# Evictions, silu and products ahead of weight splits, and level exponentials in two instructions, in a two-layer hybrid decoder trunk

## The reference

```python
def swiglu(x, w_gu, w_down):
    a, u = jnp.split(x @ w_gu, 2, axis=-1)           # 1024 -> 2 x 2816
    return (jax.nn.silu(a) * u) @ w_down             # 2816 -> 1024

# hgrn2_mixer: 4 heads of 128, by chunks, b = cumsum of log f along the tokens
att = jnp.einsum('bhtc,bhsc,bhtsc->bhts', qt, kt, decay)      # decay = exp(b_t - b_s), s <= t
o = einsum(att, vt) + einsum(qt * jnp.exp(b), state)
new_state = state * jnp.exp(b_last) + einsum(kt * jnp.exp(b_last - b), vt)

for i in range(DEPTH):                                        # DEPTH = 2
    x = layer_norm(alpha * x + 0.5 * swiglu(x, ffn_w_gu[i, 0], ffn_w_down[i, 0]), ...)
    y = token_mix(x, w_in[i], w_out[i], ...)                  # NSA | sliding window | HGRN2
    x = layer_norm(alpha * x + y, ...)
    x = layer_norm(alpha * x + 0.5 * swiglu(x, ffn_w_gu[i, 1], ffn_w_down[i, 1]), ...)
    x = x + sigmoid(x @ ple_gate_w[i] + ple_gate_b[i]) * (p[i] @ ple_w[i])
```

## Time and profile before

| what | value |
|---|---|
| median of 3 runs | 2474.37 us (2471.06 to 2482.52) |
| profiled execution, its own time | 2477.05 us |
| its span, first to last instruction | 2475.3 us |
| TensorE busy | 2312.3 us, 93% |
| VectorE busy | 1201.9 us, 49% |
| ScalarE busy | 812.4 us, 33% |
| GpSimd busy | 162.2 us, 7% |
| mean granted TensorE clock | 0.966 of 2.4 GHz |
| moved from memory | 199.33 MB, 81 GB/s |

### The profile page before, as it was taken

The page is one execution under the profiler, slowest core; times in us unless marked ns, Lnnn a source line. Parts: engine busy times, 40 slices in busy tenths (PEclk is TensorE's granted clock), DMA queues, the critical chain, the costliest instruction groups (busy, mean ns, idle before and its releaser), DMA issues.

```text
span 2475.3 us, 26371 instructions
## 1 busy us (share of the span) xinstructions
PE 2312.3 (93%) x10523; PEld 1823.0 (74%) x10523; DVE 1201.9 (49%) x1975; ACT 812.4 (33%) x1243; POOL 162.2 (7%) x142
## 2 busy tenths in 40 slices
PE   7999998999687999999999999989997789999998
PEld 6888886787355788888778888867864567888877
DVE  4333345786766433333533333367867663333444
ACT  3222224441334422222432222244413343222223
POOL 0000020220001000012000000211100010000110
PEclk9999999999789999999999999999988999999999
DMA  4333333221202233333323333332202123333321
GB/s 141 94 94 95 92 94 84 77 68 35 73 26 64 85 94 94 92 100 94 88 80 95 96 93 88 99 89 61 71 27 69 35 64 102 94 94 98 94 85 64
DMA packets 379563, 203.15 MB, mean 82 GB/s; under 512 B 8881, under 2 KB 376625, under 8 KB 379441
## 3 DMA queue, kind: packets, MB, share of 16 engines
q1 hardware_dynamic: 379440, 201.46, 28.4%
HBM read 199.33 MB, written 2.10 MB: 81 GB/s over the span
## 4 chain that ended last, share of the span: by engine, by line
PE 82%; DVE 9%; ACT 4%; issue 3%; DMA 2%; SPq 0%; POOL 0%; DVEq 0%; ACTq 0%
PE banks L240 23%; PE banks L242 23%; PE banks L241 23%; PE banks L267 2%; PE banks L268 2%; PE banks L273 2%; PE banks L773 1%; DVE w_lo L232 1%; ACT w_hi L226 1%; DVE lev L963 1%; PE banks L1179 1%; DMA w_raw<-in_ffn_w_gu_dram 1%; PE banks L1192 1%; DVE mx L1465 1%; ACT lev L1379 1%
## 5 line engine op out<-in xcount | busy, mean ns | idle before, releaser
L232 DVE TENSOR_TENSOR w_lo<-w_raw,w_hi 128x1024 fp32r<-128x1024 f32 (+2 forms) x378 | 453.9, 1203 | 967.2 <-ACT w_hi L226 966.8
L240 PE MATMUL banks<-xhi,w_hi 128*128 128x512 f32 x1888 | 761.9, 404 | 33.0 <-DVE prod L457 13.5
L241 PE MATMUL banks<-xlo,w_hi 128*128 128x512 f32 x1888 | 751.5, 398 | 0.0
L242 PE MATMUL banks<-xhi,w_lo 128*128 128x512 f32 x1888 | 750.9, 398 | 0.0
L226 ACT ACTIVATE w_hi<-w_raw 128x1024 fp32r<-128x1024 f32 (+2 forms) x378 | 376.8, 999 | 913.9 <-PE banks L242 861.8
L240 PEld LDWEIGHTS banks<-xhi,w_hi 128*128 128x128 f32 x1888 | 358.9, 190 | 128.5 <-DVE prod L457 15.3
L242 PEld LDWEIGHTS banks<-xhi,w_lo 128*128 128x128 f32 x1888 | 358.8, 190 | 86.3
L241 PEld LDWEIGHTS banks<-xlo,w_hi 128*128 128x128 f32 x1888 | 359.1, 190 | 84.6 <-issue 1.9
L240 PE MATMUL banks<-hhi,w_hi 128*128 128x512 f32 x704 | 277.3, 394 | 0.0
L242 PE MATMUL banks<-hhi,w_lo 128*128 128x512 f32 x704 | 274.1, 389 | 0.0
L241 PE MATMUL banks<-hlo,w_hi 128*128 128x512 f32 x704 | 274.0, 389 | 0.0
(11 more groups left out here) (250 smaller groups left out, 2064.0 us busy)
## 6 DMA issues: line engine op xcount, KB each, us to landing
w_raw<-in_ffn_w_gu_dram SPq DMA_DIRECT2D x176, 512.0 KB, 3.9
w_raw<-in_ffn_w_down_dram SPq DMA_DIRECT2D x64, 512.0 KB, 4.0
w_raw<-in_w_in_dram SPq DMA_DIRECT2D x52, 512.0 KB, 4.1
w_raw<-in_ffn_w_down_dram SPq DMA_DIRECT2D x32, 384.0 KB, 3.4
w_raw<-in_w_out_dram SPq DMA_DIRECT2D x32, 256.0 KB, 2.8
w_raw<-in_ple_gate_w_dram SPq DMA_DIRECT2D x16, 512.0 KB, 4.1
w_raw<-in_cmp_k_w_dram SPq DMA_DIRECT2D x8, 512.0 KB, 4.0
w_raw<-in_cmp_v_w_dram SPq DMA_DIRECT2D x8, 512.0 KB, 4.0
```

What stands on the lines that cost most here:

```text
L232: dve.tensor_tensor(part_view(wlo, n), raw_view(split_at[n]).rearrange("p k n -> p (k n)"), part_view(whi, n), ALU.subtract).then_inc(sems ...
L240: pe.matmul(bank, w_hi, x_hi, start=first, stop=False)
L241: pe.matmul(bank, w_hi, x_lo, start=False, stop=False)
L242: return pe.matmul(bank, w_lo, x_hi, start=False, stop=last)
```

## The change

The change reorders instructions of ScalarE and VectorE, in three ways.

In the feed-forward, silu(0) stands before the splits of pieces 4 and 5, product(0) before their low splits; product(1) and hidden_lo(0) stand before the low splits of pieces 6 and 7, and hidden_hi(0) before their high splits.

In the mixer, evictions (`out`) stand before the split of the same step on both engines in all steps. ScalarE's part(0, 2), which waits for VectorE's and GpSimd's subtractions, moves from step 5 to step 6, behind the high split of piece 9.

In the mixer's part 2, ScalarE's exponential over seven levels becomes two, over four and three levels, each with a semaphore increment (lev_exp); VectorE's part 3 waits for each of them in turn, and for the queries' exponential (a2) only before its last multiplication.

```diff
             for s in range(3, UP + 3 * DT):            # ffn_act
+                if s == 3:
+                    silu(0)
+                if s == 4:
+                    hidden_hi(0)
                 for n in ahead(s):
                     split_hi(act, n0 + n)
                 if s < UP and s % 2:
-                    if s == 3:
-                        silu(0)
                     silu(s // 2)
                 if s <= UP and s % 2 == 0:
-                    if s == 4:
-                        hidden_hi(0)
                     hidden_hi(s // 2 - 1)
...
+                if s == 3:                             # ffn_dve
+                    product(0)
+                if s == 4:
+                    product(1)
+                    hidden_lo(0)
                 for n in ahead(s):
                     split_lo(dve, n0 + n)
-                if s <= UP and s % 2 == 0:
-                    if s == 4:
-                        product(0)
+                if 4 < s <= UP and s % 2 == 0:
                     product(s // 2 - 1)
                 if 5 <= s <= UP + 1 and s % 2:
-                    if s == 5:
-                        hidden_lo(0)
                     hidden_lo((s - 3) // 2)
...
-                    act.activation(l2, l2, ACT.Exp)    # in_act, part 2
+                    for l0, l1 in ((0, 4), (4, LEVELS)):
+                        l2 = lev[:, LEVELS * (h % 2) + l0:LEVELS * (h % 2) + l1, :].rearrange("p l n -> p (l n)")
+                        act.activation(l2, l2, ACT.Exp).then_inc(sems["lev_exp"], 1)
...
+                if s % 2 and s > 3:                    # in_act, steps
+                    out(s - 1)
                 for m in ahead(s):
                     if m < N_IN:
                         split_hi(act, n0 + m)
-                if s % 2 and s > 3:
-                    out(s - 1)
-                if -4 <= n < STEPS and c < 3 and h + 1 < H:
+                if -4 <= n < STEPS and c < 3 and h + 1 < H and n != -2:
                     part(h + 1, c)
+                if n == -1:
+                    part(0, 2)
                 if n == -1:
                     values_out(0)
...
-                    dve.wait_ge(*upto("a2", layer, h + 1))   # in_dve, part 3
                     projected(dve, layer, T_HQ + h)
                     for lv in range(LEVELS):
+                        if lv in (0, 4):
+                            dve.wait_ge(*upto("lev_exp", layer, 2 * h + 1 + lv // 4))
                         r = pairs(level(h, lv), lv, 1)
                         dve.tensor_tensor(r, r, pairs(proj[:, T_HQ + h, :], lv, 1), ALU.mult)
+                    dve.wait_ge(*upto("a2", layer, h + 1))
                     dve.tensor_tensor(qd_of(h), qd_of(h), proj[:, T_HQ + h, :], ALU.mult).then_inc(sems["d3"], 1)
...
+                if s % 2 == 0:                         # in_dve, steps
+                    out(s - 1)
                 for m in ahead(s):
                     if m < N_IN:
                         split_lo(dve, n0 + m)
-                if s % 2 == 0:
-                    out(s - 1)
```

More of the change, by code:

```diff
@@ L120, in build @@
                 "misc_in": 16 * 4, "aux_in": 16 * 3, "rope_in": 16 * 2, "made": 4, "out_act": 13, "out_dve": 13,
-                "a0": 4, "d0": 4, "a1": 4, "d1": 4, "d2": 4, "p2": 4, "a2": 4, "d3": 4, "c_mm": 16, "att_done": 16,
+                "a0": 4, "d0": 4, "a1": 4, "d1": 4, "d2": 4, "p2": 4, "lev_exp": 8, "a2": 4, "d3": 4, "c_mm": 16, "att_done": 16,
                 "b4_mm": 17, "b4_out": 17, "st_mm": 12, "st_out": 12, "pv_done": 16, "o_raw": 4, "sq_done": 4, "ms_mm": 4,
@@ L881, in part @@
                     act.wait_ge(*upto("p2", layer, h + 1))
-                    l2 = lev[:, LEVELS * (h % 2):LEVELS * (h % 2) + LEVELS, :].rearrange("p l n -> p (l n)")
-                    act.activation(l2, l2, ACT.Exp)
+                    for l0, l1 in ((0, 4), (4, LEVELS)):
+                        l2 = lev[:, LEVELS * (h % 2) + l0:LEVELS * (h % 2) + l1, :].rearrange("p l n -> p (l n)")
+                        act.activation(l2, l2, ACT.Exp).then_inc(sems["lev_exp"], 1)
                     act.activation(kd_of(h), kd_of(h), ACT.Exp)
```

## The result

The changed kernel takes 2438.49 us (median of 4 runs, 2430.07 to 2439.68), the kernel before 2474.52 us (4 runs, 2471.06 to 2482.52). The ratio is 0.9848, with a 95% interval of 0.9828 to 0.9868: 1.5% faster. The forecast was 2437 us.

What follows compares the result with a forecast made beforehand. TensorE, busy 93% of the span, was taken as the bound, with its idle time and lower clock to gain. 21.4 + 14.8 + 1.6 - 0.2 = 37.6 us off the median 2474.37 us gave 2437 us, range 2430 to 2452.

Steps and rivals of the forecast that it cites:

- Feed-forward openings, 21.4 us: Four feed-forward openings: TensorE's waits for the product (13.5 us) and the slow pieces behind them (7.9 us) go.
- clock term: Feed-forward openings: the four pieces behind the waits, slow at a lowered clock, return to 5.58 us; 7.9 us gained.
- Mixer openings, 14.8 us: Both layers' mixer openings: TensorE's waits for piece 5's eviction (6.1 and 4.3 us) and the slow pieces behind them go.
- The later waits, 1.6 us: Later in each mixer: TensorE's 0.81 us wait for an eviction behind a low split goes; 1.6 us for both layers.
- VectorE's lead, 0.2 us taken and 5.6 us kept for the range: Mixers: the next head's subtractions may run beside GpSimd's, returning up to 2.8 us of waits per layer; 0.2 us taken.
- The exponentials in two instructions, nothing: Mixer part 2: splitting the level exponential is worth about nothing; the first head's part 3 is just on time without it.
- The prediction's check on the span: Span shorter by 5 us at the first feed-forward stage's end, by 13 to 14 us in layer 0's attention heads.
- Rival C: Attention heads: shifted phase drops the clock for good, 77 us lost per layer; at half of it 2514 us; chance 0.02.
- A: Openings: waits go but the clock falls nevertheless, so 12.3 us of slow pieces stay; 2449 us; chance 0.10.
- D: A moved instruction waits for something as late as before; with the feed-forward part void, 2458 us; chance 0.06.
- B: Mixers: VectorE becomes the bound and sets the pace, 5.8 us lost per layer; 2448 us; chance 0.10.

Runs made afterwards that it cites:

- one that takes back the clock term alone: Kernel before, with 20 matmuls of constants run by TensorE during each feed-forward opening's wait for the product: 2465.82 us, ratio 0.9963.
- one that removes both: Kernel before with only the feed-forward part of the change, the mixer as before: 2453.34 us, ratio 0.9903.
- the other three kernels that have the wait: Kernel before with the mixer's new order alone (2456.41 us), two exponentials alone (2474.85 us), or piece 5's eviction alone moved ahead (2465.16 us).
- both kernels that separate them: Kernel before with the level exponential in two instructions alone: 2474.85 us, ratio 0.9997; changed kernel with one level exponential: 2437.72 us, ratio 0.9842.
- The filler behind the norms: Changed kernel with TensorE multiplying constants while awaiting the first tile behind a norm (34 matmuls in four waits, 18 in two): 2427.61 us, ratio 0.9802.

## Why the prediction was right

**Feed-forward openings, 21.4 us.** Read from the starts of piece 3 and piece 5, the four openings became 5.2, 5.2, 6.5 and 5.1 us shorter (the first: 16.33 us before, 38.61 to 49.76 after), 22.0 us in all. The split into a wait (13.5 us) and a clock term (7.9 us) is shown by two kernels, one that takes back the clock term alone and one that removes both: with the wait's time kept and TensorE at work the ratio gives 9 us, with an interval of 6 to 12, and the openings 6.9; with the wait gone it gives 24 us, with an interval of 20 to 28. One thing in the clock term is luck: 2.9 of its 7.9 us are the one piece of 8.48 us, a value that did not come again in the twelve openings of the other three kernels that have the wait; by theirs the term would be 5.1 to 6.4 us.

**Mixer openings, 14.8 us.** From piece 3 to piece 8 layer 0 took 38.78 us and takes 30.61 (419.03 to 449.64), 8.2 us less for 7.9 forecast; layer 1 took 37.77 and takes 30.71 (1623.39 to 1654.10), 7.1 for 6.9. The eviction runs at 440.62, right behind the small copy, as the prediction put it, and piece 7 follows the turns without a gap:

```profile
440.52 0.18 DVE L1071 COPY pos_t<-banks 128x32 f32<-128x32 f32 x1
440.62 0.68 DVE L939 COPY proj<-banks 128x512 f32<-128x512 f32 x1
```

**The later waits, 1.6 us.** They are gone, and were worth 2.1 us. The remaining 1.1 us of waits for evictions are the two of 0.55 us at the very start of the mixers, as said.

**VectorE's lead, 0.2 us taken and 5.6 us kept for the range.** The head's levels did run more beside GpSimd's: 4.21 us against 3.29, GpSimd's seven starting 3.4 us before VectorE's. That is 0.9 of the 2.8 us bound; in layer 1 it is 3.75 us against 3.29. From 418 to 600 TensorE waits 0.5 us in all, so it cost nothing. The rows:

```profile
461.11 4.21 DVE L967 TENSOR_TENSOR lev<-cum 128x256 f32<-128x256 f32 x7
```

```profile
457.72 6.32 POOL L1090 TENSOR_TENSOR lev<-cum,karg 128x256 f32<-128x256 f32 x7 [18.00 <-DVE karg L960]
```

One subtraction of the seven beside GpSimd, and one behind GpSimd's last, which ends at 464.03:

```profile
462.70 0.85 DVE L967 TENSOR_TENSOR lev<-cum 128x256 f32<-128x256 f32 x1
```

```profile
464.24 0.41 DVE L967 TENSOR_TENSOR lev<-cum 128x256 f32<-128x256 f32 x1
```

So a subtraction beside GpSimd's takes about twice the time of one alone, and the size of the term follows from their number: two of the seven before (3.29 us), four now (4.21), all seven in the first head (6.09). The prediction's bound of 2.8 us would need all seven, but GpSimd is halfway through its own when VectorE begins. Whether the two engines' instructions exclude each other one by one, as the Trainium skill's page "SBUF — State Buffer" that the prediction cites has it, was not tried; by that rule the prediction had the 5.6 us due, and they did not come, for the overlap was short.

**The exponentials in two instructions, nothing.** Shown by both kernels that separate them. Part 3 ends 0.3 us early without them, where the working had it just on time, and 2.0 us early with them, where it had 1.5.

**What the sum left out.** The span fell by 37.8 us. The openings and the later waits give 22.0 + 8.2 + 7.1 + 2.1 (the later pieces' starts moved by 1.1 and 1.0 us more) = 39.4 us; the start of the program was 1.3 us later in this execution (piece 3 at 38.61 instead of 37.28); the second stage of heads took 5.9 us more, as shown above. The remaining 5.6 us are a balance of gains and losses in stretches where no instruction moved. Of the gains 3.8 us lie behind the two norms ahead of the embeddings, from the norm's last matmul to the first piece behind the opening: 23.46 and 23.50 us before, at a clock of 0.85, and 22.32 and 20.80 now, at 0.92 and 1.00. So the nearness of forecast and result, 1.5 us, is in part luck: what the unchanged stages lost and what they gained at other clocks happened to cancel. The prediction's check on the span shows it too. It wanted 13 to 14 us less in the attention heads of layer 0; it is 11.4 at their start and 11.8 at their end, for the start of the program was 1.3 us later and 2.3 us went back at the end of the mixer, where the clock was 0.79 instead of 1.00. At the end of the first feed-forward stage it is 3.8 us less, not 5, by the same late start.

Rival C had named the stage of heads rightly as the place that can move, and its size wrongly: over the ten profiles of this study (nine kernels and the kernel before, none of which changes the stage) its length lies between 171 and 178 us in either layer, with 38 to 58 us of it at the lower clock. That is a spread of some 7 us for each layer, and the likely source of the spread of the runs: of the changed kernel's four runs the one of 2430.07 us has a mean clock of 0.973, the three of 2437.67 to 2439.68 have 0.967 to 0.969. Nor does the order of the change as such lower that clock: in the changed kernel with one exponential the two stages take 173.3 and 174.1 us. Why the clock of the stage differs from one profile to another was not settled.

**Rivals A and D** are out: the pieces run at 1.00, and both parts give what they should. **B** named a mechanism that exists (VectorE's lead shrank), but TensorE's steps have more slack than it needs.

## What to carry to other kernels

Where engines run in program order, the instruction that another engine waits for belongs ahead of all work that is only needed later, even where that work is ready first; look for the one instruction that is late (here one product and one eviction), since the moves around it may be worth nothing, as in the feed-forward openings, or a few us, as in the mixer. In these profiles a wait of TensorE of 3.1 to 6.1 us cost its own length and then, in all but two cases, 1.4 to 2.9 us of a slow piece, so count both, and the second as a range; the two waits of 1.9 and 1.1 us before the mixer's products had no such piece behind them. Where the wait could not be removed, matmuls of constants into a free bank that just filled it gave back the second part.

## What was not expected

The filler behind the norms gives 11 us (ratio 0.9802 against 0.9848), about a third of what the whole change gives, for three lines and a constant on one engine. Matmuls of 384 columns with a new weight load for each came at 0.18 us (20 in 3.58 us), which is three quarters of the 0.233 us of a matmul of 512 columns in a piece, but at 0.19 us behind the norm (34 in 6.46 us).
